# The opening of a float32 transformer block on one core: tokens also fetched as rows, four weight units in pieces, the strip product moved

## The chip, the cores and the metric

The kernel runs on one core of one Trainium2 chip. The metric is the device time of one execution in microseconds (us), the median of several runs.

## What is computed, cut to what matters

The input x has 512 tokens of 1024 channels, mem has 256 rows of 1024. The block is: a gated mixer with a short convolution, a long one and attention over mem; a convolutional feed-forward; an RMS norm; then a second layer of sliding-window attention with sinks and a bias per distance; a last RMS norm. The opening that the change touches computes this much of it:

```python
h    = rmsnorm(x, norm_mix_g)            # x * rsqrt(mean(x*x) + 1e-6) * g, over 1024 channels
memn = rmsnorm(mem, norm_mem_g)
k, v = split(memn @ w_kv)                # 256 x 2048
proj = h @ w_in                          # everything else of the mixer reads h
bias = t5_table[t5_bucket(distance)]     # second layer: one number per head and distance
```

## The kernel before, in words

**Units.** All weights stream from HBM in units of 128 x 1024 float32 (512 KB), four units a round, 54 rounds. Unit i uses slot i % 4 of three buffers: raw (w_raw), high (w_high) and low (w_low). Each float32 matmul is made of three with rounded operands: high x high, high x low of the activations, and low x high. ScalarE (ACT) makes the high part by a copy that rounds (round_high, L474; called by unit_high in the opening), VectorE (DVE) the low part by a subtraction (take_low, L1237; unit_low), TensorE (PE) multiplies. Channels lie on the partitions, tokens along the row, so x is eight tiles of 128 x 512 (x_in) and mem eight of 128 x 256.

**Who orders the work.** Every engine has a list written by hand and is in order; semaphores join them. SyncE (SP) issues the weights: in round m the load of slot s waits until the low part of the unit that had the slot is made (weight_low, L406). ACT's cast of unit i waits for its landing and until PE is done with unit i - 4 (unit_done). Nothing is reordered at run time: a step that waits holds up all that stands behind it on its engine.

**The opening.** Units 0 to 2 arrive in four pieces (CHUNKS) of 384 KB, each with two k tiles of all three units; mem arrives on ACT's queue in four pieces of 256 KB, with 4 KB of gains between, and 254 KB of other parameters behind. Unit 3 arrives whole. For each piece ACT rounds the three weight pieces (L519) and scales and rounds two tiles of mem (L525), DVE makes the low parts (L1326, L1332). PE runs four warm-up products of zeros (L964), then for each k tile nine matmuls of 256 columns (key_part, L927), and units 3 to 7 whole (key_unit, L939). Keys are divided by mem's norm later (take_k, L1350). The squares of mem are summed over tiles by ACT (L533) and DVE (L1343), and over channels by PE transposes (total, L909) and a DVE reduction. For x the same is done with eight squares on ACT (x_squares, L539), seven additions on DVE (add_x_squares, L1365) and four transposes on PE (L909, from part). spread (L917) turns the inverse roots back. Units 8 to 15 are the values (value_slab, L956). Meanwhile DVE scales the tiles of x (x_tiles: scale_tile L1274, low_tile L1279) and ACT rounds them (x_high, L505). The first round that reads h is two(R_LONG, 0, ...) (L872): it starts when units 16 and 17 are rounded and h's tiles arrive one by one. From there on PE has one long stream of products.

**The strip.** The distance bias of the second layer is a product of two small tables (L1089), made between the halves of the down projection, copied by DVE (L1675), stored by GpSimd (POOL), expanded in HBM, and read back.

Of the kernel before, what the change touches and what calls it, by code (L numbers as in the profile page):

```python
# [63 lines left out]
EARLY = 3  # L64
# [22 lines left out]
for _name, _n in (("g_mem", KT), ("g_mix", KT), ("long_w", KT * TAPS), ("long_b", KT), ("ln_g", KT), ("ln_b", KT),  # L87
                  ("gate_b", 3 * KT), ("short_w", 3 * KT), ("g_ffn", KT), ("ffn_w", 3 * 2 * F_TILES),
                  ("g_final", KT), ("g_second", KT), ("g_last", KT), ("sinks", HEADS_B)):
    PARAMS[_name] = _at  # L90
    _at += _n
# [6 lines left out]
def build(nc, weights, x, mem, params, consts, table, onehot, rows_g, out):  # L98
    with ExitStack() as ctx:
# [39 lines left out]
        mem_in = sb("mem_in", [P, KT, MEM], F32, 161)  # L139
        k_mem = sb("k_mem", [P, KT, MEM], F32, 161)  # L140
# [11 lines left out]
        x_sq = sb("x_sq", [P, KT, SEQ], F32, 64)  # L152
# [58 lines left out]
        strip = part[0:HEADS_B, 0, 0:2 * P]  # L211
        onehot_sb = convs[0:32, 0, 0:2 * P]
        table_sb = convs[0:32, 0, 2 * P:2 * P + HEADS_B]
        x_sum = part[:, 0, :]
# [17 lines left out]
        landed = [sem(f"weights_landed{s}") for s in range(SLOTS)]  # L232
        first_landed = [sem(f"first_landed{c}") for c in range(CHUNKS)]
        chunk_high = sem("chunk_high")
# [10 lines left out]
        x_squared = sem("x_squared")  # L245
        x_added = sem("x_added")
        gain_landed = sem("gain_landed")
# [114 lines left out]

        def stats(norm, n):


            return (slice(4, 4 + n), 2) if norm == N_MEM else (slice(0, n), 3)
# [29 lines left out]
        def _(sp):  # L396
            for c in range(CHUNKS):
# [4 lines left out]
            for s in range(EARLY, SLOTS):  # L402
                sp.dma_start(raw[s][:, :], weights[s]).then_inc(landed[s], 16)

            def load(m, s):
                sp.wait_ge(weight_low, 4 * m + (s - 3))  # L406
# [4 lines left out]

            load_x(0)
            load_x(1)
            load(1, 0)
            load(1, 1)
            load_x(2)
            load(1, 2)
            load_x(3)
            load(1, 3)
            with sp.Fori(2, ROUNDS) as m:  # L420
# [9 lines left out]
        def _(pool):  # L430
            pool.memset(conv_sum, 0.0).then_inc(zeros_set, 1)
            pool.dma_start(ones, consts[:, 0:P]).then_inc(consts_landed, 16)
# [3 lines left out]

            pool.wait_ge(ln_low, KT)
# [3 lines left out]
            pool.dma_start(table_sb, table).then_inc(tables_landed, 16)  # L441
            pool.dma_start(onehot_sb, onehot).then_inc(tables_landed, 16)
            pool.dma_start(own_keys[:, :], consts[:, 2 * P:3 * P]).then_inc(masks_landed, 16)
            pool.dma_start(older_keys[:, :], consts[:, 3 * P:4 * P]).then_inc(masks_landed, 16)
            pool.wait_ge(strip_ready, 1)
            pool.dma_start(strip_dram[:, :], strip).then_inc(strip_stored, 16)
            pool.wait_ge(strip_stored, 16)

# [16 lines left out]
        def _(act):  # L465
            def round_high(m, s):
# [3 lines left out]

                act.wait_ge(landed[s], 16 * m + (16 if s >= EARLY else 0))

                at_least(act, unit_done, 4 * m + (s - 3))
                act.activation(w_high[:, s, :], raw[s][:, :], ACT.Copy).then_inc(weight_high, 1)  # L474
# [32 lines left out]
            def load_memory(c):  # L507
                act.dma_start(mem_in[:, 2 * c:2 * c + 2, :], mem[:, 2 * c:2 * c + 2, :]).then_inc(mem_landed[c], 16)

            load_memory(0)  # L510
            act.dma_start(par[:, 0:KT], params[:, 0:KT]).then_inc(gain_landed, 16)
            for c in range(1, CHUNKS):
                load_memory(c)
            act.dma_start(par[:, KT:N_PARAMS], params[:, KT:N_PARAMS]).then_inc(par_landed, 16)
            for c in range(CHUNKS):
                act.wait_ge(first_landed[c], 16)
                for s in range(EARLY):
                    at = c * CHUNK
                    act.activation(w_high[:, s, at:at + CHUNK], raw[s][:, at:at + CHUNK], ACT.Copy)\  # L519
# [1419 lines left out]
```

## Time and profile before

| | us |
|---|---|
| three runs | 1213.33, 1213.44, 1213.69 |
| median | 1213.44 |
| profiled execution: its time | 1213.84 |
| profiled execution: its span | 1212.1 |
| PE busy | 1203.7 (99%) |
| DVE busy | 827.7 (68%) |
| ACT busy | 490.3 (40%) |

The span runs from the first to the last instruction of one profiled execution; its time has what lies around the span too. Busy time is summed per engine, and PE's matmuls overlap a little at their ends.

### The profile page before, as it was taken

How to read it: one execution, taken by the hardware profiler on the slowest of the kernel's cores; microseconds unless marked ns; L12 is line 12 of the kernel's file. 1: busy time of each engine (PE TensorE's matmuls, PEld its weight loads, DVE VectorE, ACT ScalarE, POOL GpSimd, SP SyncE). 2: the span in 40 equal slices, each digit the busy share in tenths (PEclk: the TensorE clock that was granted, in tenths of full speed). 3: DMA queues.
4: the chain of work that ended last, by engine and by line, in shares of the span. 5: the costliest groups of instructions: out<-in, count | busy, mean ns of one | idle time of the engine just before them, and what ended most of it. 6: DMA issues, size and time to landing. Idle time of an engine off the chain costs nothing.

```text
span 1212.1 us, 15930 instructions
## 1 busy us (share of the span) xinstructions
PE 1203.7 (99%) x5656; PEld 994.3 (82%) x5656; DVE 827.7 (68%) x1293; ACT 490.3 (40%) x785; POOL 7.5 (1%) x18
## 2 busy tenths in 40 slices
PE   9999999999999999999999999999999999999998
PEld 8888888888888888888887888888888888887786
DVE  6868897797889987553367866566654444578762
ACT  7544333232333323552244534334333333155643
POOL 0000000000000000000000000000000000000000
PEclk9999999999999999999999999999999999999999
DMA  8533222222222232243322222223233434221211
GB/s 321 179 104 104 87 104 83 74 87 87 70 87 90 100 105 87 87 174 104 104 87 87 90 104 92 96 104 104 87 110 104 174 104 139 87 71 53 74 66 70
DMA packets 35841, 125.51 MB, mean 104 GB/s; under 512 B 4080, under 2 KB 5760, under 8 KB 35536
## 3 DMA queue, kind: packets, MB, share of 16 engines
q1 hardware_dynamic: 33424, 116.41, 27.7%
q0 software_dynamic: 928, 6.08, 1.4%
q10 hardware_dynamic: 1440, 2.36, 0.5%
q8 instruction: 32, 0.52, 0.2%
q14 instruction: 17, 0.14, 0.0%
HBM read 122.72 MB, written 4.21 MB: 105 GB/s over the span
## 4 chain that ended last, share of the span: by engine, by line
PE 99%; DMA 0%; DVE 0%; ACT 0%; issue 0%; ACTq 0%; DVEq 0%
PE acc L855 80%; PE acc L872 3%; PE side L1203 2%; PE acc L1203 2%; PE acc L877 1%; PE acc L939 1%; PE side L1129 1%; PE acc L1167 1%; PE acc L892 1%; PE side L1005 1%; PE side L1025 1%; PE side L956 1%; PE acc L956 1%; PE acc L927 1%; PE acc L1139 1%; DMA par<-params 0%
## 5 line engine op out<-in xcount | busy, mean ns | idle before, releaser
L1237 DVE TENSOR_TENSOR w_low<-w_raw,w_high 128x1024 fp32r<-128x1024 f32 x213 | 257.6, 1221 | 42.1 <-ACT w_high L474 38.9
L474 ACT ACTIVATE w_high<-w_raw 128x1024 fp32r<-128x1024 f32 x213 | 221.0, 1051 | 103.2 <-PE acc L855 86.9
L855 PE MATMUL acc<-h_high,w_high 128*128 128x512 f32 x880 | 218.2, 390 | 0.0
L855 PE MATMUL acc<-h_low,w_high 128*128 128x512 f32 x880 | 217.4, 389 | 0.0
L855 PE MATMUL acc<-h_high,w_low 128*128 128x512 f32 x880 | 217.4, 390 | 0.0
L855 PEld LDWEIGHTS acc<-h_low,w_high 128*128 128x128 f32 x880 | 165.2, 188 | 34.3
L855 PEld LDWEIGHTS acc<-h_high,w_low 128*128 128x128 f32 x880 | 165.2, 188 | 34.2
L855 PEld LDWEIGHTS acc<-h_high,w_high 128*128 128x128 f32 x880 | 164.6, 188 | 33.8
L1312 DVE SCALAR_TENSOR_TENSOR convs<-long_u,par,convs 128x510 f32<-128x510 f32 (+28 forms) x232 | 170.4, 734 | 6.6
L1522 DVE TENSOR_TENSOR gate<-acc,gate 128x512 f32<-128x512 f32 x16 | 11.1, 692 | 53.7 <-PE acc L855 52.1
L855 PE MATMUL acc<-f_high,w_high 128*128 128x512 f32 x176 | 43.9, 390 | 0.0
L855 PE MATMUL acc<-f_low,w_high 128*128 128x512 f32 x176 | 43.8, 389 | 0.0
L855 PE MATMUL acc<-f_high,w_low 128*128 128x512 f32 x176 | 43.8, 389 | 0.0
L1654 DVE TENSOR_TENSOR x<-acc,x 128x512 f32<-128x512 f32 x8 | 5.5, 692 | 54.5 <-PE acc L855 54.5
L855 PEld LDWEIGHTS acc<-f_high,w_high 128*128 128x128 f32 x176 | 33.0, 188 | 7.2 <-issue 0.4
L855 PEld LDWEIGHTS acc<-f_high,w_low 128*128 128x128 f32 x176 | 33.0, 188 | 6.9
L855 PEld LDWEIGHTS acc<-f_low,w_high 128*128 128x128 f32 x176 | 33.0, 188 | 6.9
L635 ACT ACTIVATE ya_high<-part 128x512 fp32r<-128x512 f32 x8 | 5.1, 632 | 71.6 <-DVE part L1497 71.6
L738 ACT ACTIVATE square<-x 128x512 f32<-128x512 f32 x8 | 5.1, 632 | 70.8 <-DVE x L1654 70.8
L722 ACT ACTIVATE f_high<-part 128x512 f32 (+1 forms) x22 | 13.9, 632 | 48.3 <-DVE part L1636 48.3
L855 PE MATMUL acc<-xn_high,w_high 128*128 128x512 f32 x128 | 33.0, 400 | 0.0
L500 ACT ACTIVATE gate<-acc,par 128x512 f32<-128x512 f32 x24 | 16.5, 686 | 40.1 <-PE acc L855 40.0
(337 smaller groups left out, 1705.2 us busy)
## 6 DMA issues: line engine op xcount, KB each, us to landing
w_raw<-weights SPq DMA_DIRECT2D x213, 512.0 KB, 3.2
x_in<-x SPq DMA_DIRECT2D x4, 512.0 KB, 10.3
x<-x POOLq DMA_DIRECT2D x1, 2048.0 KB, 8.5
rows_dram<-strip_dram POOLq DMA_DIRECT2D x1, 2048.0 KB, 11.7
w_raw<-weights SPq DMA_DIRECT2D x4, 384.0 KB, 7.2
mem_in<-mem ACTq DMA_DIRECT2D x4, 256.0 KB, 7.3
bias<-rows_dram POOLq DMA_DIRECT2D x1, 1024.0 KB, 7.1
out<-result ACTq DMA_DIRECT2D x4, 256.0 KB, 2.6
```

What stands on the lines that cost most here:

```text
L474: act.activation(w_high[:, s, :], raw[s][:, :], ACT.Copy).then_inc(weight_high, 1)
L500: act.activation(gate[:, half, :], acc[:, 2 * half, :], ACT.Sigmoid, bias=0.0 if bias_col is None else bias_col).then_inc(taken[2 * half], 1)
L722: act.activation(f_high[:, j, :], part[:, half, :], ACT.Copy).then_inc(ffn_high, 1)
L855: mm = pe.matmul(acc[:, bank, 0:width], w[:, s, (skip + b) * P:(skip + b + 1) * P], moving[v][:, k, :], start=first and b == 0 and w is w_ ...
L872: pe.matmul(acc[:, s + i, 0:width], w_high[:, s + i, k * P:(k + 1) * P], moving[v][:, k, :], start=k == 0 and v == 0, stop=False)
L877: mm = pe.matmul(acc[:, s + i, 0:width], w_low[:, s + i, k * P:(k + 1) * P], moving[0][:, k, :], start=False, stop=k == KT - 1)
L892: mm = pe.matmul(acc[:, s + t // half, at:at + 2 * P], still[v][:, k, t * P:(t + 1) * P], w[:, s:s + 2, k * P:(k + 1) * P], start=k == 0 a ...
L927: mm = pe.matmul(acc[:, s, at:at + MEM], w[:, s, k * P:(k + 1) * P], memory[v][:, k, :], start=k == 0 and w is w_high and v == 0, stop=k = ...
L956: mm = pe.matmul(dst, o[:, k, t * P:(t + 1) * P], w[:, i, c * SEQ:(c + 1) * SEQ], start=k == 0 and o is mem_high and w is w_high, stop=k = ...
L1203: mm = pe.matmul(bank, o[:, k, t * P:(t + 1) * P], w[:, s, half * SEQ:(half + 1) * SEQ], start=False, stop=k == KT - 1 and o is o2_low)
L1237: dve.tensor_tensor(w_low[:, s, :], raw[s][:, :], w_high[:, s, :].bitcast(F32), ALU.subtract)\
L1312: dve.scalar_tensor_tensor(conv_acc[:, shift:SEQ], long_u[:, tile, 1:SEQ + 1 - shift], w, conv_acc[:, shift:SEQ], ALU.mult, ALU.add).then_ ...
```

## The change

In the opening all four units of the first round now arrive in pieces (EARLY is 4). Their first pieces of two k tiles are transfers of their own, 128 KB each, one per unit; the later three groups are 512 KB each. The very first weight piece is rounded by DVE instead of ACT. mem's gains are put in front of its first tile in one transfer (mem_first, 132 KB); the second tile and the next two come on ACT's queue, the other four on SP's between the weight groups; the 254 KB of parameters move to SP's queue, behind unit 9. PE's order within a group is unit by unit instead of tile by tile, and each pass waits for its own operands only. Units 4 and 5 get buffers of their own (w_spare), so that they are loaded without waiting for slots 0 and 1. Two of four warm-up products stay.

x is fetched a second time as rows, tokens on the partitions (x_rows, 2 MB, in SP's queue between units 8 and 9). ACT squares a row and sums along it in one instruction with accum_out (four of 128 x 1024). The eight squares, seven additions, PE's four transposes and DVE's reduction for x go.

The strip product runs on PE after the first group; its tables are POOL's first transfer, ACT copies the result and POOL stores it then. The order of the later steps of the opening on ACT, DVE and PE is rewritten.

The diff, cut to its core (from the third part on the added lines; unchanged and removed ones are left out):

```diff
 CHUNKS = 4
-EARLY = 3
+EARLY = SLOTS
+SPARE = 2
...
+        w_spare = sb("w_spare", [P, SPARE, UNIT], F32, 56)
+        x_rows = sb("x_rows", [P, SEQ // P, D], F32, 64)
...
+        def raw_of(m, s):
+            return w_spare[:, s, :] if isinstance(m, int) and m == 1 and s < SPARE else raw[s][:, :]
...
+        def mem_tile(k):
+            return mem_in[:, k, :] if k else mem_first[:, KT:KT + MEM]
...
+        def folds(norm):
...
+            return norm + (3 if norm == N_MEM else 2)
...
+            for s in range(EARLY):
+                sp.dma_start(w_raw[:, s, 0:CHUNK], weights[s, :, 0:CHUNK]).then_inc(alone_landed[s], 16)
+            for c in range(1, CHUNKS):
...
+                if c < CHUNKS - 1:
+                    tiles = slice(2 * c + 2, 2 * c + 4)
+                    sp.dma_start(mem_in[:, tiles, :],
+                                 mem[:, KT:KT + KT * MEM].rearrange("p (k n) -> p k n", k=KT)[:, tiles, :])\
+                      .then_inc(mem_landed[c + 1], 16)
+            for s in range(SPARE):
+                sp.dma_start(w_spare[:, s, :], weights[SLOTS + s]).then_inc(spare_landed[s], 16)
...
+            def load(m, s, units=None):
+                sp.wait_ge(weight_low, 4 * m + (s - 3) if units is None else units)
...
+            def load_rows(i):
+                sp.dma_start(x_rows[:, 2 * i:2 * i + 2, :],
+                             x_tokens.rearrange("(t p) d -> p t d", p=P)[:, 2 * i:2 * i + 2, :])\
+                  .then_inc(x_rows_landed[i], 16)
...
+            load(1, 2)
+            load(1, 3)
+            load(2, 0, 1)
+            load_rows(0)
+            load_rows(1)
+            load(2, 1, 2)
+            sp.dma_start(par[:, :], params).then_inc(par_landed, 16)
...
+            load(2, 2)
...
+            load(2, 3)
+            with sp.Fori(3, ROUNDS) as m:
...
+            pool.dma_start(tables_sb, tables).then_inc(tables_landed, 16)
...
+            act.dma_start(mem_first[:, :], mem[:, 0:KT + MEM]).then_inc(mem_first_landed, 16)
+            act.dma_start(mem_in[:, 1, :], mem[:, KT + MEM:KT + 2 * MEM]).then_inc(mem_landed[0], 16)
+            act.dma_start(mem_in[:, 2:4, :], mem[:, KT + 2 * MEM:KT + 4 * MEM].rearrange("p (k n) -> p k n", k=2))\
+               .then_inc(mem_landed[1], 16)
...
+                    if c or s:
+                        act.wait_ge(first_landed[c] if c else alone_landed[s], 16)
+                        act.activation(w_high[:, s, at:at + CHUNK], raw[s][:, at:at + CHUNK], ACT.Copy)\
+                           .then_inc(chunk_high if c < CHUNKS - 1 else weight_high, 1)
+                    if s == 0:
+                        for k in range(2 * c, 2 * c + 2):
+                            act.wait_ge(mem_landed[c] if k else mem_first_landed, 16)
+                            act.activation(mem_high[:, k, :], mem_tile(k), ACT.Copy, scale=mem_first[:, k:k + 1])\
+                               .then_inc(act_high, 1)
+            act.wait_ge(strip_done, 1)
+            act.activation(strip, side[0:HEADS_B, 2, 0:2 * P], ACT.Copy).then_inc(strip_ready, 1)
...
+            def x_squares(*tiles):
...
+                for t in tiles:
+                    act.wait_ge(x_rows_landed[t // 2], 16)
+                    act.activation(x_rows[:, t, :], x_rows[:, t, :], ACT.Square, accum_out=stat_col[:, t:t + 1])\
+                       .then_inc(x_summed, 1)
...
+            unit_high(4, 5, 6, 7, 8)
...
+            x_squares(0, 1)
+            unit_high(9)
+            x_squares(2, 3)
+            root(N_X)
...
+            unit_high(12)
+            x_high(2)
+            unit_high(13)
+            x_high(3)
+            unit_high(14)
+            x_high(4)
...
+            unit_high(15)
+            x_high(5)
+            unit_high(16)
+            x_high(6)
+            unit_high(17)
...
+            def key_part(c, i, by_tile):
...
+                passes = [(k, o) for k in range(2 * c, 2 * c + 2) for o in range(3)] if by_tile else \
+                    [(k, o) for o in range(3) for k in range(2 * c, 2 * c + 2)]
+                for k, o in passes:
+                    if o == 0:
+                        if c == 0 and i == 0:
+                            pe.wait_ge(first_high, 1)
+                        else:
+                            at_least(pe, *((chunk_high, EARLY * c + i) if c < CHUNKS - 1 else (weight_high, i + 1)))
+                        pe.wait_ge(act_high, k + 1)
+                    if o == 1:
+                        pe.wait_ge(act_low, k + 1)
+                    if o == 2:
+                        at_least(pe, *((chunk_low, EARLY * c + i + 1) if c < CHUNKS - 1 else (weight_low, i + 1)))
+                    w, v = ((w_high, 0), (w_high, 1), (w_low, 0))[o]
...
+                                   start=k == 0 and o == 0, stop=k == KT - 1 and o == 2)
+                if c == CHUNKS - 1:
...
+            for width in (SEQ, SEQ):
...
+            for c in range(CHUNKS):
...
+                    key_part(c, i, c == 0 and i == 0)
+                if c == 0:
+                    pe.wait_ge(tables_landed, 16)
+                    pe.matmul(side[0:HEADS_B, 2, 0:2 * P], tables_sb[:, 2 * P:2 * P + HEADS_B], tables_sb[:, 0:2 * P],
+                              start=True, stop=True).then_inc(strip_done, 1)
+            key_unit(4)
...
+            for i in range(5, KT):
+                key_unit(i)
...
+                if norm == N_X:
+                    dve.wait_ge(x_summed, n)
+                else:
+                    dve.wait_ge(stat_done, folds(norm))
+                    add_rows(cols, bank, n).then_inc(total_read, 1)
+                    dve.wait_ge(total_read, folds(norm))
...
+            dve.wait_ge(alone_landed[0], 16)
+            dve.tensor_copy(w_high[:, 0, 0:CHUNK], raw[0][:, 0:CHUNK]).then_inc(first_high, 1)
...
+                    if c == 0 and s == 0:
+                        dve.wait_ge(first_high, 1)
+                    elif c < CHUNKS - 1:
+                        dve.wait_ge(chunk_high, EARLY * c + s)
...
+                    for k in range(2 * c, 2 * c + 2) if s == 0 else ():
+                        dve.wait_ge(act_high, k + 1)
+                        dve.scalar_tensor_tensor(mem_low[:, k, :], mem_tile(k), mem_first[:, k:k + 1],
+                                                 mem_high[:, k, :].bitcast(F32), ALU.mult, ALU.subtract)\
+                           .then_inc(act_low, 1)
...
+            for c in range(1, CHUNKS):
+                add_mem_squares(c)
...
+            unit_low(4, 5, 6)
...
+            unit_low(7, 8, 9)
...
+            unit_low(10)
...
+            take_k(2, 6)
+            unit_low(11)
+            take_k(3, 7)
...
+            x_tiles(0, 1, 2)
+            unit_low(12)
+            x_tiles(3)
+            unit_low(13)
+            take_k(0, 4)
+            x_tiles(4)
+            unit_low(14)
+            x_tiles(5)
+            take_k(1, 5)
+            unit_low(15)
+            x_tiles(6, 7)
+            unit_low(16)
...
+            unit_low(17)
```

## Rows read from the trace of the kernel before

**Rows 1.** The page: chain that ended last, and the DMA issues of weight units.
```profile
PE 99%; DMA 0%; DVE 0%; ACT 0%; issue 0%; ACTq 0%; DVEq 0%
...
w_raw<-weights SPq DMA_DIRECT2D x213, 512.0 KB, 3.2
```

**Rows 2.** Timeline of PE and its weight loads (PEld): start, duration, count.
```profile
1.32 5.88 PE L964 MATMUL side<-convs 128*128 128x512 f32 x8 [1.32 <-POOL convs L431]
...
4.05 0.34 PEld L964 LDWEIGHTS side<-convs 128*128 128x128 f32 x1 [0.52 <-issue]
...
6.60 0.19 PEld L964 LDWEIGHTS side<-convs 128*128 128x128 f32 x1 [0.51 <-issue]
...
8.23 0.36 PE L927 MATMUL acc<-mem_high,w_high 128*128 128x256 f32 x1 [1.03 <-DVE mem_low L1332]
...
19.81 1.12 PE L939 MATMUL acc<-mem_high,w_high 128*128 128x256 f32 x8
...
31.54 0.60 PE L909 MATMUL side<-ident_sb,part 128*128 128x128 f32 x4
31.98 0.38 PE L917 MATMUL side<-ident_sb,root_col 128*128 128x128 f32 x2
...
54.81 0.47 PE L872 MATMUL acc<-h_high,w_high 128*128 128x512 f32 x1 [0.18 <-ACT w_high L474]
```

**Rows 3.** Timeline of PE around the strip product.
```profile
950.28 0.60 PE L1089 MATMUL side<-convs 32*16 32x256 f32 x2
950.81 2.11 PE L855 MATMUL acc<-f_high,w_high 128*128 128x512 f32 x8
```

**Rows 4.** Windows: stretch, length, busy us by engine, PE clock, DMA share, GB/s.
```profile
5.00:10.00 5.00, 3.96 (x20) 2.56 (x19) 3.49 (x10) 4.07 (x11) 0.00 (x0) 1.00 1.04 360
10.00:15.00 5.00, 5.00 (x44) 5.00 (x43) 4.25 (x11) 4.28 (x11) 0.00 (x0) 1.00 1.05 400
15.00:20.00 5.00, 5.00 (x44) 5.00 (x43) 3.78 (x5) 4.76 (x9) 0.00 (x0) 1.00 0.97 351
20.00:25.00 5.00, 5.00 (x44) 5.00 (x44) 4.31 (x6) 3.72 (x6) 0.00 (x0) 1.00 1.02 414
...
35.00:40.00 5.00, 5.00 (x26) 4.20 (x25) 4.96 (x8) 1.11 (x2) 0.00 (x0) 1.00 0.63 214
40.00:45.00 5.00, 5.00 (x24) 4.14 (x23) 5.00 (x10) 2.68 (x4) 0.00 (x0) 1.00 0.34 97
```

**Rows 5.** DMA issues at 0.75, 0.76, 1.24, 2.84 and 16.61: KB, us to landing.
```profile
w_raw<-weights SPq DMA_DIRECT2D x1, 384.0 KB, 4.9
mem_in<-mem ACTq DMA_DIRECT2D x1, 256.0 KB, 4.4
...
par<-params ACTq DMA_DIRECT2D x1, 4.0 KB, 5.7
...
w_raw<-weights SPq DMA_DIRECT2D x1, 512.0 KB, 11.0
...
w_raw<-weights SPq DMA_DIRECT2D x1, 512.0 KB, 8.9
```

**Rows 6.** Timeline of ACT and its queue (ACTq).
```profile
1.79 1.62 ACTq L508 DMA_DIRECT2D mem_in<-mem  x3
...
5.68 1.03 ACT L519 ACTIVATE w_high<-w_raw 128x256 fp32r<-128x256 f32 x3 [0.38 <-DMA w_raw<-weights]
6.98 0.91 ACT L525 ACTIVATE mem_high<-mem_in,par 128x256 fp32r<-128x256 f32 x2 [0.27 <-DMA par<-params]
...
15.24 2.18 ACT L533 ACTIVATE mem_sq<-mem_in 128x512 f32<-128x512 f32 x4
...
52.61 1.99 ACT L474 ACTIVATE w_high<-w_raw 128x1024 fp32r<-128x1024 f32 x2
```

**Rows 7.** Timeline of DVE: units 10 and 11, and the scaling of tile 6.
```profile
35.82 2.35 DVE L1237 TENSOR_TENSOR w_low<-w_raw,w_high 128x1024 fp32r<-128x1024 f32 x2
...
51.30 0.74 DVE L1274 SCALAR_TENSOR_TENSOR part<-x_in,par,side 128x512 f32<-128x512 f32 x1
```

More of the change, by code:

```diff
@@ L95, with build @@
 N_MEM, N_X, N_LN, N_FFN, N_FINAL, N_LAST = range(-2, 4)
-def build(nc, weights, x, mem, params, consts, table, onehot, rows_g, out):
+def build(nc, weights, x, x_tokens, mem, params, consts, tables, rows_g, out):
     with ExitStack() as ctx:
@@ L210, in build @@
         ffn_y = [gate[:, 0, :], gate[:, 1, :], conv_acc, conv_sum]
[L211 to L214, printed above, removed]
+        strip = probs[0:HEADS_B, 0, :]
+        tables_sb = convs[0:32, 0, 0:2 * P + HEADS_B]
         rstd_mem = gate[:, 0, 0:MEM]
@@ L232, in build @@
         landed = [sem(f"weights_landed{s}") for s in range(SLOTS)]
+        alone_landed = [sem(f"alone_landed{s}") for s in range(EARLY)]
         first_landed = [sem(f"first_landed{c}") for c in range(CHUNKS)]
+        spare_landed = [sem(f"spare_landed{s}") for s in range(SPARE)]
+        first_high = sem("first_high")
+        mem_first_landed = sem("mem_first_landed")
+        x_rows_landed = [sem(f"x_rows_landed{i}") for i in range(2)]
+        x_summed = sem("x_summed")
         chunk_high = sem("chunk_high")
@@ L469, in round_high @@
                     return
-                act.wait_ge(landed[s], 16 * m + (16 if s >= EARLY else 0))
+                if isinstance(m, int) and m == 1 and s < SPARE:
+                    act.wait_ge(spare_landed[s], 16)
+                else:
+                    act.wait_ge(landed[s], 16 * m - (16 if s < SPARE else 0))
                 at_least(act, unit_done, 4 * m + (s - 3))
-                act.activation(w_high[:, s, :], raw[s][:, :], ACT.Copy).then_inc(weight_high, 1)
+                act.activation(w_high[:, s, :], raw_of(m, s), ACT.Copy).then_inc(weight_high, 1)
             def ahead(m, s):
@@ L1086, in _ @@
             down_body(0)
-            pe.wait_ge(tables_landed, 32)
-            pe.matmul(side[0:HEADS_B, 2, 0:2 * P], table_sb, onehot_sb, start=True, stop=True)\
-              .then_inc(strip_done, 1)
             down_body(1)
@@ L1673, in _ @@
             down_body(0)
-            dve.wait_ge(strip_done, 1)
-            dve.tensor_copy(strip, side[0:HEADS_B, 2, 0:2 * P]).then_inc(strip_ready, 1)
             down_body(1)
```

148 lines of the change are left out of this document (21 added, 127 removed).

## The prediction

> **What bounds the kernel now.** I read four views, in this order. The page's chain that ended last is 99% TensorE (PE) [rows 1]. So a change of the opening pays only through PE: a later or earlier first useful matmul, PE work removed, PE waits removed or added. PE's order of time shows where its stream begins: warm-up matmuls from 1.32 to 7.20 us, the first useful matmul at 8.23, then no gap until 54.81, where the first round that reads h (L872) waits 0.18 us for ScalarE's (ACT's) cast of a weight unit [rows 2]. Third, the other engines beside it: VectorE (DVE) is busy 4.96 and 5.00 us of the two 5 us stretches from 35 to 45 us [rows 4]; it is nearly the bound there, and the 0.18 us wait is its shadow, since ACT's cast of units 16 and 17 stands behind a tile of h that DVE has to scale. Fourth, the DMA view: the core's queues are full, 400 and 414 GB/s, in the stretches from 10 and from 20 us [rows 4].
>
> This makes three clocks: PE's, the DVE/ACT chain's, and that of the loads. The kernel before is paced by the first, with the second 0.2 us behind. The profiled execution took 1213.84 us around its span of 1212.1; the median of the three runs is 1213.44. Sums are made against the profiled one, then 0.40 is taken off.
>
> **PE's own gains.** (a) The transposes of the sum of x squares go: from 31.54 to the next group at 31.98, 0.44 us [rows 2]. (b) The strip product leaves the down projection: its two instructions stand between 950.28 and 950.81, 0.53 us [rows 3]. It is added after the first pieces in the opening. There PE will wait anyway (below), so I cost it at nothing there; without that cover it costs the same 0.53 back, and (b) is zero. (c) The number of key and value matmuls is the same, 192 and 96 groups' worth, only in another order.
>
> **PE's start.** Now the first matmul waits for the whole first piece of three units and for the 4 KB of gains, which landed 5.7 us after their issue at 1.24, hence 6.95; then come two ACT steps (the first from 6.98) and two of DVE [rows 5, 6]. After the change the first transfers are 128 and 132 KB instead of 384 and 256 KB; these landed 4.9 and 4.4 us after issue [rows 5], at 5.65 and 5.16. With a third of the bytes ahead I take 4.1 us for both. Bounds: an uncontended 512 KB unit lands 3.2 us after issue [rows 1], of which 1.27 are its bytes at 414 GB/s; a quarter of the bytes would land at 0.75 + 1.9 + 0.3 = 3.0; no gain gives 5.2. ACT's table load is out of the way by then, because ACT issues three transfers ahead of it instead of six, at 0.54 us each [rows 6]. One DVE copy of 0.4 and one ACT piece of 0.5 follow, and the two warm-up matmuls (four instructions of 0.85 us, from 1.32 [rows 2]) end at 4.75. First matmul: 4.85 us, 3.4 earlier.
>
> **What of this lasts.** PE then needs the pieces in time. Before the second group of pieces is complete, 1024 KB on SP's queue, 516 on ACT's and 163 on POOL's must land, 1703 KB. Before the fourth group it is 3239 KB (2560 on SP's). Before the change unit 3 landed at 2.84 + 11.0 = 13.84 [rows 5] behind 3458 KB (2048, 1282, 128). The 219 KB less are 0.55 us at 400 GB/s: fourth group at 13.3. The second stands 1536 KB (1.57 MB) ahead of it; at 360 to 400 GB/s [rows 4] that is 4.1 us: 9.2, and adding up the rate rows forwards gives 8.5; I take 9.0. Group 1 keeps PE busy until about 8.6, and then it waits, with the strip product inside the wait. ACT needs for a group four weight pieces at 0.34 and two of mem at 0.46 [rows 6], 2.2 us, so ACT ends groups 2 to 4 at 11.2, 13.4 and 15.6. PE needs 24 matmuls at 0.12 (96 took from 8.23 to 19.81 [rows 2]) = 2.88 us a group. Its first unit of group 2 is done at about 11.2, a step behind ACT's and DVE's pieces of mem; the other three units end at 13.4, group 3 at 16.3, group 4 at 19.2. Unit 4 is the next wait. Its cast now stands behind the strip copy (0.4) and all squares of mem (2.4, four took 2.18 [rows 6]): 15.6 + 2.8 + 1.05 = 19.5. Before, unit 4 began at 19.81 [rows 2]. So of 3.4 us only 0.3 are left here. With (a), PE would be ready for the h round at 54.63 - 0.3 - 0.44 = 53.9.
>
> **What the loads allow.** The change adds 2 MB (x again, as rows), in SP's queue ahead of units 9, 10 and 11, and moves the 254 KB of parameters there. Unit 6 is loaded when three units' low parts are done: ACT's third piece of group 4 plus DVE's 0.42, about 15.7 us; POOL's queue is not in the way, as it only issues its 163 KB first and then waits for the strip. An uncontended unit lands 3.2 us after issue [rows 1]: 18.9. From there to the landing of unit 11 are 13.5 pieces of 512 KB (units 7 to 11: 5, rows 4, x 4, parameters 0.5). Two prices for one: at 414 GB/s, the rate from 20 to 25 us [rows 4], 1.27 us; from landing to landing, 13.84 to 16.61 + 8.9 = 25.51 for eight pieces [rows 5], 1.46, which has a dip of the rate in the 5 us from 15 in it (351 GB/s [rows 4]). I take 1.31, the 400 GB/s row, because it is the nearest stretch with one queue full and no dip; 17.7 us, so unit 11 lands at 36.6 (36.0 to 38.6).
>
> The Trainium skill, page "DMA: Bandwidth & Descriptors", section "Anatomy of one DMA — SWDGE (gpsimd) path", gives 436 GB/s for the part that grows with size. By it a piece is 1.20 us, unit 11 lands at 35.1 and the sum below would end PE-bound. The trace's best 5 us show 414.
>
> **What DVE then needs.** DVE takes unit 11's low part ahead of every tile of h, in an in-order queue. Before, from the start of unit 10's low part (35.82) to the scaling of tile 6 (51.30) it ran 15.48 us without a gap: six low parts, six scalings, five h lows, four K tiles [rows 7]. After, from unit 11's: one low part less (1.14), two K tiles more (0.67): 15.0. From that scaling the way to PE was ACT's h tile, two casts, and PE at 54.81 [rows 2, 6]; with the new interleave it is one cast: 52.61 + 1.05 + 0.21 - 51.30 = 2.6. With the cast of unit 11 ahead (1.1) the h round starts 18.7 us after unit 11 has landed: 36.6 + 18.7 = 55.3. That DVE no longer adds x squares (seven of them) doesn't help: this work lay before the landing, and the time becomes idling for weights. ACT's squares of rows (four of twice the length, for eight at 0.54) lie there too.
>
> **Sum.** The h round starts at 55.3 instead of 54.81: +0.5. Afterwards PE's stream is as before, its loads are far ahead, and the strip is out: -0.53. Together 0.0. The other moves cost nothing: the strip's store and POOL's early wait lie 140 us ahead of the first reader (attend), which has one more satisfied wait; mem's gains travel with mem. 1213.84 + 0.0 - 0.40 = 1213.4; with the landing at 36.0, which the 1.27 price gives, it is 1212.8, and I take 1213.3.
>
> **Rivals.**
> 1. PE stays the pace: the loads keep up (unit 11 by 35.2 or earlier) and the whole gain of the opening stays. Then the h round starts when PE is ready, 53.9: -0.91 - 0.53 = -1.4, so 1212.0; if the second group lands at 8.0 instead of 9.0 and ACT follows, one more us, 1211.0. For it: 414 GB/s over five us, and a DVE with spare time before 33 us. Against: 2 MB ahead of weights in one queue, and a gap of about 1 us in the queue before unit 6. Chance 0.28; a third of it is beyond 2.4 us.
> 2. The other side: the loads fall behind. At 1.46 us a piece unit 11 lands at 38.6, the h round starts at 57.3: +2.5 - 0.53 = +2.0, so 1215.4; it decides once a piece takes over 1.31. Past 1.49 it is slower by over 0.2%. For it: the measured eight landings. Chance 0.14, half of it past the bound.
> 3. The clock. The first warm-up instructions (512 columns) start 0.85 us apart (three between 4.05 and 6.60) and their weight loads take 0.34 us; the one at 6.60 takes 0.19 [rows 2], as do all later ones. That is the step from 1.2 to 2.4 GHz, although the granted-clock column shows 1.00 throughout [rows 4]; PE had been busy for about 5 us. The change halves this warm-up and follows it with matmuls that wait. At 1.2 GHz a 256-column matmul takes 0.21 instead of 0.12. Group 1 slow costs 24 x 0.09 = 2.2 us, of which a third is covered by the wait for group 2, and what is left by the 1.4 us that PE waits at the h round; only when group 2 is slow too is PE late, by 2 us: 1215.3. The Trainium skill, page "TensorE: Matmul & The Clock Gate", Part 1, says that the low level is the default and activity lifts it, which speaks against cutting the warm-up; by that rule, the trace agrees that it began low. Chance 0.08, a third of it past the bound.
> 4. The strip product isn't covered, or the squares of rows are late for the spread at about 33.5 us: some tenths, inside the range.
>
> **How the numbers follow.** The forecast case (loads gate the h round, 1212.4 to 1214.2) has 0.50, rivals 1, 2, 3 have 0.28, 0.14, 0.08. A measurement of this kernel can tell about 0.2%, 2.4 us, from no change. Faster by more: a third of rival 1 and a bit, 0.10. Slower by more: half of rival 2 and a third of 3, 0.10. Within: 0.80. The range reaches from rival 1's far end, 1211.2, to rival 2's 1215.3.
>
> **What would show it.** First matmul near 4.9 us; a PE wait of 0.5 to 1 us before its second group; unit 4 at about 19.5; no L909 from part; DVE idle 5 us or more between 24 and 37 us behind casts that wait for DMA; unit 11's landing at 36 to 37; a wait of over 1 us at the h round for ACT's cast, at about 55.3; no strip instruction near 950. Wrong if PE's wait at the h round is absent (rival 1), if the landing is past 38 (rival 2), or if weight loads of 0.34 us are still seen after 9 us (rival 3).

## The result, and the profile after

| | before | after |
|---|---|---|
| median of 15 runs each, us | 1213.47 (1213.33 to 1214.14) | 1215.58 (1215.03 to 1216.68) |
| ratio, 95% interval | | 1.0019 (1.0012 to 1.0025) |
| profiled execution: time, span, us | 1213.84, 1212.1 | 1215.88, 1214.1 |
| first useful matmul, us | 8.23 | 4.70 |
| unit 4 on PE, us | 19.81 | 19.15 |
| first round that reads h, us | 54.81 | 57.66 |

The kernel became 2.1 us slower. That is a little less than the 2.4 us (0.2%) which the prediction took as the least that one measurement can tell, but it is outside the predicted range (1211.2 to 1215.3) by 0.3 us. The interval of the ratio lies above 1, so the loss is real.

The page's chain of the kernel after, which answers to [rows 1], and then PE's waits (engine, line, releaser: us in all, times, longest):

```profile
PE 95%; DMA 2%; DVE 2%; ACT 1%; issue 0%; SPq 0%; DVEq 0%; ACTq 0%
```

```profile
PE acc L1007 <- ACT w_high L509: 1.8, 1, 1.8
...
PE acc L912 <- ACT w_high L509: 1.2, 1, 1.2
...
PE side L1007 <- ACT w_high L509: 0.3, 1, 0.3
```

Before, 99% of the chain was PE. Now 5% lie elsewhere, 2% of the span with the loads of weights: DMA, ACT's cast and DVE's low part have become links of the chain. All three waits are for a cast of a weight unit. The timeline of PE says when; it answers to [rows 2] and [rows 3]:

```profile
1.32 3.78 PE L1015 MATMUL side<-convs 128*128 128x512 f32 x4 [1.32 <-POOL convs L464]
4.70 0.61 PE L978 MATMUL acc<-mem_high,w_high 128*128 128x256 f32 x1
...
9.21 0.60 PE L1021 MATMUL side<-convs 32*16 32x256 f32 x2
9.96 0.76 PE L978 MATMUL acc<-mem_high,w_high 128*128 128x256 f32 x2
...
19.15 1.12 PE L990 MATMUL acc<-mem_high,w_high 128*128 128x256 f32 x8
...
40.23 1.19 PE L1007 MATMUL side<-w_high,mem_high 128*128 128x512 f32 x4 [0.30 <-ACT w_high L509]
...
45.08 1.20 PE L1007 MATMUL acc<-w_high,mem_high 128*128 128x512 f32 x4 [1.83 <-ACT w_high L509]
...
57.66 0.47 PE L912 MATMUL acc<-h_high,w_high 128*128 128x512 f32 x1 [1.23 <-ACT w_high L509]
```

The front of the opening is what was forecast: the useful work starts 3.5 us earlier, and of that 0.66 us are left at unit 4. Everything is lost between 40 and 58 us, in three waits of 3.4 us together: 0.30 at unit 11, 1.83 at unit 12 and 1.23 at the h round (the first round that reads h). The ledger against the kernel before has three entries. The h round starts 57.66 - 54.81 = 2.85 us later. By 949 us 0.09 of that has worn off: the product at 951.36 is the one that stood at 948.60 before. Then the strip's two instructions are missing. Before the change, first, and after it, these are the products around the place (those at 950.28 and 950.81 are in [rows 3]):

```profile
948.60 1.75 PE L855 MATMUL acc<-f_high,w_low 128*128 128x512 f32 x7
...
952.76 1.98 PE L855 MATMUL acc<-f_low,w_high 128*128 128x512 f32 x8
```

```profile
951.36 1.75 PE L895 MATMUL acc<-f_high,w_low 128*128 128x512 f32 x7
952.95 1.98 PE L895 MATMUL acc<-f_high,w_high 128*128 128x512 f32 x8
954.76 1.98 PE L895 MATMUL acc<-f_low,w_high 128*128 128x512 f32 x8
```

The same products take 3.40 us now and took 4.16, so the strip was worth 0.76 us there, not only the 0.53 between its own start and the next product's. The sum is 2.85 - 0.09 - 0.76 = +2.0, by which the spans differ.

Why the casts are late shows on ACT and DVE, after (start, duration; the bracket is the idle time before and what ended it). The three casts are those of units 9, 10 and 11, the low part is unit 11's:

```profile
29.50 1.06 ACT L509 ACTIVATE w_high<-w_raw 128x1024 fp32r<-128x1024 f32 x1 [1.63 <-DMA w_raw<-weights]
...
35.28 1.06 ACT L509 ACTIVATE w_high<-w_raw 128x1024 fp32r<-128x1024 f32 x1 [1.99 <-DMA w_raw<-weights]
39.12 1.06 ACT L509 ACTIVATE w_high<-w_raw 128x1024 fp32r<-128x1024 f32 x1 [2.78 <-DMA w_raw<-weights]
```

```profile
40.21 1.22 DVE L1280 TENSOR_TENSOR w_low<-w_raw,w_high 128x1024 fp32r<-128x1024 f32 x1 [1.49 <-ACT w_high L509]
...
42.02 1.40 DVE L1320 SCALAR_TENSOR_TENSOR part<-x_in,par,side 128x512 f32<-128x512 f32 x2
```

Each cast starts within 0.1 us of its unit's landing. DVE stands behind unit 11 too: only after its low part does it scale the first tile of h, at 42.02. Before the change unit 11's low part was done at 38.2, since it is the second of the two that start at 35.82 [rows 7]. SP's queue and the issue of unit 11 (KB, us to landing) close the chain backwards:

```profile
15.87 2.35 SPq L430 DMA_DIRECT2D w_raw<-weights  x3
18.26 0.94 SPq L436 DMA_DIRECT2D x_rows<-x_tokens  x2
```

```profile
w_raw<-weights SPq DMA_DIRECT2D x1, 512.0 KB, 14.0
```

Unit 11 is issued at 25.05 and lands at 39.05. Before the change a unit in the full queue took 8.9 and 11.0 us [rows 5]. The windows of 2 us around SP's issue show one more thing; the columns are those of [rows 4]:

```profile
12.00:14.00 2.00, 2.00 (x19) 2.00 (x19) 2.00 (x7) 1.96 (x7) 0.00 (x0) 1.00 1.06 394
14.00:16.00 2.00, 2.00 (x19) 2.00 (x18) 2.00 (x7) 2.00 (x7) 0.00 (x0) 1.00 0.50 199
16.00:18.00 2.00, 2.00 (x19) 2.00 (x18) 1.06 (x3) 2.00 (x6) 0.51 (x1) 1.00 0.58 152
18.00:20.00 2.00, 2.00 (x19) 2.00 (x19) 1.86 (x4) 2.00 (x4) 0.00 (x0) 1.00 0.87 258
```

From 14 to 20 us only 199, 152 and 258 GB/s move, where the stretches around show 394 and 398. The queue has run dry: a shorter window shows that nothing moves from 15.5 to 16.0, and it fills again only slowly.

```profile
15.50:16.00 0.50, 0.50 (x6) 0.50 (x6) 0.50 (x3) 0.50 (x3) 0.00 (x0) 1.00 0.00 0
```

SP stands at the load of unit 6, which waits for the low parts of three units (weight_low) until 15.87. Behind it in SP's list are the 2 MB of rows, which wait for nothing.

### The profile page after: what moved, and what is told of

It reads as the page before. It is cut to its first block, busy times and chain, and to the rows that moved or that the text cites. A ratio compares the mean times of both kernels' runs of the same rounds, so it can differ in the third digit from the quotient of the medians.

```text
span 1214.1 us, 15903 instructions
## 1 busy us (share of the span) xinstructions
PE 1203.3 (99%) x5648; PEld 993.5 (82%) x5648; DVE 823.1 (68%) x1288; ACT 491.2 (40%) x789; POOL 7.0 (1%) x17
## 4 chain that ended last, share of the span: by engine, by line
PE 95%; DMA 2%; DVE 2%; ACT 1%; issue 0%; SPq 0%; DVEq 0%; ACTq 0%
PE acc L895 80%; PE acc L912 3%; DMA w_raw<-weights 2%; PE side L1246 2%; PE acc L1246 2%; PE acc L917 1%; PE side L1172 1%; PE acc L1210 1%; PE acc L932 1%; PE side L1052 1%; PE side L1072 1%; DVE w_low L1280 1%; PE acc L1182 1%; PE side L1062 0%; DVE part L1320 0%
## 5 line engine op out<-in xcount | busy, mean ns | idle before, releaser
L1280 DVE TENSOR_TENSOR w_low<-w_raw,w_high 128x1024 fp32r<-128x1024 f32 x210 | 254.3, 1221 | 45.9 <-ACT w_high L509 42.6
L509 ACT ACTIVATE w_high<-w_raw 128x1024 fp32r<-128x1024 f32 x210 | 218.4, 1051 | 107.9 <-PE acc L895 86.2
L1563 DVE TENSOR_TENSOR gate<-acc,gate 128x512 f32<-128x512 f32 x16 | 11.1, 692 | 53.7 <-PE acc L895 52.2
```

The source lines that it names most:

```text
L509: act.activation(w_high[:, s, :], raw_of(m, s), ACT.Copy).then_inc(weight_high, 1)
L1280: dve.tensor_tensor(w_low[:, s, :], raw_of(m, s), w_high[:, s, :].bitcast(F32), ALU.subtract)\
```

## Experiments, first set: what sets the h round

The theory after the result was that the h round is unit 11's landing plus a fixed chain, and that the landing is late by 2 MB in a queue that had been empty for some microseconds. The rivals were a slow clock after the halved warm-up, and ACT's list (the squares of the rows stand ahead of the casts).

**rows_first** issues the rows ahead of the waiting load.

```diff
+            load_rows(0)
+            load_rows(1)
             load(1, 2)
             load(1, 3)
             load(2, 0, 1)
-            load_rows(0)
-            load_rows(1)
```

> Both transfers of x as rows (2 MB) are issued before the load of unit 6, which waits for weight_low 3; nothing else changes. Load theory (the queue runs empty from about 15.3 to 18 us while SP stands at that wait, and the landing of unit 11 sets the h round 18.6 us later): the queue stays full, unit 11 lands about 2.3 us earlier, at 36.8 instead of 39.1, PE's waits before units 10 and 12 go, the h round starts at 55.4 instead of 57.66, the time falls by 2.2 us to 1213.4; unit 6 lands near 22 instead of 19.8, which PE doesn't need before 24.9. Clock theory (the loss is matmuls at 1.2 GHz at the start): no change, 1215.6.

Measured: 1213.31 us (1213.03 to 1213.75, 11 runs), ratio 0.9999 (0.9990 to 1.0008). The move of two lines gives back the whole loss. First the same windows of 2 us, then from the timeline ACT's cast of unit 11, DVE's low part of it, and PE's h round:

```profile
14.00:16.00 2.00, 2.00 (x19) 2.00 (x18) 2.00 (x6) 2.00 (x7) 0.00 (x0) 1.00 1.03 412
16.00:18.00 2.00, 2.00 (x19) 2.00 (x18) 1.06 (x3) 2.00 (x6) 0.51 (x1) 1.00 1.03 410
18.00:20.00 2.00, 2.00 (x19) 2.00 (x19) 1.86 (x4) 1.91 (x3) 0.00 (x0) 1.00 1.02 403
```

```profile
35.69 1.06 ACT L509 ACTIVATE w_high<-w_raw 128x1024 fp32r<-128x1024 f32 x1 [0.31 <-DMA w_raw<-weights]
...
37.68 1.22 DVE L1280 TENSOR_TENSOR w_low<-w_raw,w_high 128x1024 fp32r<-128x1024 f32 x1
...
55.12 0.47 PE L912 MATMUL acc<-h_high,w_high 128*128 128x512 f32 x1 [0.92 <-ACT w_high L509]
```

The dip is gone, and unit 11 is cast 3.4 us earlier. The h round gains only 2.5 us: now 2.0 us pass between that cast and DVE's low part, without a wait of DVE, where in the kernel after it was 1.1. So another gate has come up close behind the landing. Unit 6 lands later (cast at 23.53, after 3.62 us of waiting), and PE doesn't notice. So units 6 to 8 need not go ahead of the rows.

**half_rows** takes 1 MB of rows, two pieces of 512 KB, out of the queue. ACT squares the rows of the first half a second time in place of those of the second (into a buffer rows_out, which is new), so its work is the same and the statistics of the second half of the tokens are left out. **extra_load** puts 512 KB more in, behind the rows, into a buffer that no product reads (ACT waits for it behind the values, long after it has landed).

```diff
-            load_rows(1)
...
-                    act.wait_ge(x_rows_landed[t // 2], 16)
-                    act.activation(x_rows[:, t, :], x_rows[:, t, :], ACT.Square, accum_out=stat_col[:, t:t + 1])\
+                    act.wait_ge(x_rows_landed[0], 16)
+                    act.activation(x_rows[:, t, :] if t > 1 else rows_out[:, t, :], x_rows[:, t % 2, :], ACT.Square, accum_out=stat_col[:, t:t + 1])\
```

> Only the first half of x as rows is fetched (1 MB less ahead of units 9 to 11); the squares of token tiles 2 and 3 are taken from tiles 0 and 1 again, so the statistics of the second half of the tokens are left out. Work on every engine is the same. Load theory: unit 11 lands 2.6 us earlier, at 36.5, the h round starts at about 55.1, time 1213.1. Clock theory: no change, 1215.6. If the cost were ACT's squares of rows and not the bytes: no change either.

```diff
             load_rows(1)
+            sp.dma_start(extra[:, :], weights[8]).then_inc(extra_landed, 16)
             load(2, 1, 2)
```

> One more 512 KB transfer (a copy of unit 8 into an unused buffer) behind the rows in SP's queue. Load theory: each later landing moves by 1.3 to 1.4 us and passes to the end one to one: 1216.9. Theory that PE or DVE work bounds the opening: no change, 1215.6.

Measured, both 0.5 us above what was expected: half_rows 1213.61 us (1212.55 to 1214.15), ratio 1.0001 (0.9992 to 1.0010); extra_load 1217.36 (1216.67 to 1217.91, 6 runs), ratio 1.0032 (1.0020 to 1.0045). Their casts of unit 11 and h rounds, first half_rows and then extra_load:

```profile
37.12 1.06 ACT L509 ACTIVATE w_high<-w_raw 128x1024 fp32r<-128x1024 f32 x1 [4.31 <-DMA w_raw<-weights]
...
55.70 0.47 PE L912 MATMUL acc<-h_high,w_high 128*128 128x512 f32 x1 [1.26 <-ACT w_high L509]
```

```profile
41.19 1.06 ACT L512 ACTIVATE w_high<-w_raw 128x1024 fp32r<-128x1024 f32 x1 [2.77 <-DMA w_raw<-weights]
...
59.73 0.47 PE L916 MATMUL acc<-h_high,w_high 128*128 128x512 f32 x1 [1.22 <-ACT w_high L512]
```

ACT's work is the same in half_rows and the loss is gone all the same, so the squares of the rows aren't the cause; the bytes are.

**warm4** has the four warm-up products of the kernel before.

```diff
-            for width in (SEQ, SEQ):
+            for width in (SEQ, SEQ, SEQ, MEM):
```

> All four warm-up products again, so PE is busy with them until about 7.2 us and starts the first group 2.4 us later, at 2.4 GHz. Load theory: PE starts late but the h round still waits for unit 11, 57.7: time within 0.3 us of 1215.6, PE's waits before units 10, 12 and the h round shorter by what it starts later. Clock theory: the slow matmuls go, faster by 1 us or more, 1214.6 or less.

Measured: 1215.70 us (1214.83 to 1216.81), ratio 1.0020 (1.0011 to 1.0029); unit 4 at 19.26. It is as slow as the kernel after, so the clock of the first microseconds isn't the cause. PE's first useful matmul comes at 6.26, not 2.4 us later than in the kernel after but 1.6, and the strip, right behind group 1, at 9.40 instead of 9.21: what PE loses by the later start, it gets back by the faster products.

The four kernels in one table (us; the last column is the h round less the start of DVE's low part of unit 11):

| | cast of unit 11 | h round | difference | from DVE's low part |
|---|---|---|---|---|
| half_rows | 37.12 | 55.70 | 18.58 | 17.48 |
| after | 39.12 | 57.66 | 18.54 | 17.45 |
| extra_load | 41.19 | 59.73 | 18.54 | 17.45 |
| rows_first | 35.69 | 55.12 | 19.43 | 17.44 |

The landing moves over 4 us and the h round follows it one for one. In warm4 (and in strip_twice, below) SP's list is that of the kernel after, and yet unit 11 is cast at 38.77 and 38.54; the h rounds, at 57.31 and 57.09, are again 18.54 and 18.55 us behind. So the landing itself differs by 0.6 us between executions of one list, and differences of that size between these kernels say nothing of their edits. In rows_first the cast no longer decides, but DVE's low part still does, to 0.04 us. The chain from there on is DVE's own work, as [rows 7] said.

## Experiments, second set: the next gate, and a better version

In rows_first the landing of unit 11 cost only 0.31 us. The theory was now that the lists of ACT, DVE and PE hold the casts of units 10 and 11 back. In the kernel after, the casts wait for PE to be done with unit i - 4, ACT has the last two squares and the root of x between the casts of units 9 and 10, and DVE takes x's mean between the low parts of 9 and 10.

**loads_only** improves only SP's list further (x after units 10 and 11 where it can), with the other lists as they are.

```diff
+            load_rows(0)
+            load_rows(1)
             load(1, 2)
             load(1, 3)
             load(2, 0, 1)
-            load_rows(0)
-            load_rows(1)
             load(2, 1, 2)
...
+            load(2, 2)
             load_x(0)
+            load(2, 3)
             load_x(1)
-            load(2, 2)
             load_x(2)
             load_x(3)
-            load(2, 3)
```

> On top of rows_first the loads of units 10 and 11 also move ahead of most of x in SP's queue; ACT, DVE and PE keep the order of the changed kernel. Load theory taken alone (unit 11's landing sets the h round): unit 11 lands about 3.5 us earlier than in rows_first, near 32, so the h round would start when PE is ready, 54.2, and the time would be 1212.4. List theory (once the queue is full, ACT's list is next: unit 10 is cast only after four squares and the root, so DVE starts its low part at 35.4 as in rows_first): the h round stays at about 55.1, time 1213.3.

Measured: 1213.24 us (1213.17 to 1213.79), ratio 1.0000 (0.9991 to 1.0009). ACT, DVE and PE of this kernel:

```profile
34.19 1.99 ACT L509 ACTIVATE w_high<-w_raw 128x1024 fp32r<-128x1024 f32 x2
...
37.53 1.22 DVE L1280 TENSOR_TENSOR w_low<-w_raw,w_high 128x1024 fp32r<-128x1024 f32 x1
...
54.97 0.47 PE L912 MATMUL acc<-h_high,w_high 128*128 128x512 f32 x1 [0.91 <-ACT w_high L509]
```

ACT now casts 10 and 11 back to back and waits for no transfer, and yet they begin at 34.19: both units lie ready. The h round is 17.44 us after DVE's low part once more. Earlier landings alone gain nothing more that can be measured; the lists hold.

**reordered** adds to loads_only what the lists need: all four squares of rows right after unit 5, both roots after unit 8, both means together on DVE, and PE's spread of x's root ahead of the first value slab.

```diff
-            unit_high(4, 5, 6, 7, 8)
-            root(N_MEM, MEM // P)
-            x_squares(0, 1)
-            unit_high(9)
-            x_squares(2, 3)
-            root(N_X)
-            unit_high(10, 11)
+            unit_high(4, 5)
+            x_squares(0, 1, 2, 3)
+            unit_high(6, 7, 8)
+            root(N_MEM, MEM // P)
+            root(N_X)
+            unit_high(9, 10, 11)
...
-            value_slab(0, 0)
             spread(N_X, SEQ)
+            value_slab(0, 0)
...
             mean_square(N_MEM, MEM)
-            unit_low(7, 8, 9)
             mean_square(N_X, SEQ)
+            unit_low(7, 8, 9)
             unit_low(10)
```

> As loads_only, and ACT squares all four row tiles right after unit 5, takes both roots after unit 8, DVE makes both mean squares together, PE spreads x's roots ahead of unit 8's product. The work is the same. List theory: DVE reaches the tiles of h some 3 us earlier, PE is the pace with no wait at the h round, which starts at about 53.7: -1.1 against before there and -0.53 for the strip: 1211.8. If some other bound lies behind (PE's own start, DVE's sum of work), the h round stays near 55 and the time above 1213.

Measured: 1211.89 us (1211.49 to 1213.13), ratio to the kernel before 0.9988 (0.9979 to 0.9997). It is faster than both kernels: 3.7 us less than after, 1.5 less than before. The cast of unit 11, and PE at the h round:

```profile
33.62 1.06 ACT L509 ACTIVATE w_high<-w_raw 128x1024 fp32r<-128x1024 f32 x1 [2.37 <-DMA w_raw<-weights]
...
52.72 1.07 PE L1006 MATMUL acc<-w_low,mem_high 128*128 128x512 f32 x4
53.62 0.39 PE L911 MATMUL acc<-h_high,w_high 128*128 128x512 f32 x1
```

There is no bracket at 53.62: PE goes from the last product of the values straight into the h round, and PE is the bound again. What PE still waits for behind its first product is 0.25 us at group 2 and 0.24 us at unit 6. The cast of unit 11 waits for its landing again, but 33.62 + 18.54 is 52.2, and PE isn't ready before 53.62. The four moves came together; no run shows which of them could be left out.

**reordered_warm4** is that kernel with four warm-up products, since the clock might have been covered by the waits until now.

> As reordered, with four warm-up products instead of two. Here PE should be the pace, so that a PE start that is later, but at 2.4 GHz, can show. Clock theory: faster than reordered by 0.3 us or more. Theory that the wait for the second group of pieces absorbs either: equal within 0.2 us.

Measured: 1211.82 us (1211.47 to 1212.23), ratio 0.9987 (0.9978 to 0.9996): no different from reordered. PE starts group 1 at 5.89 instead of 4.63, the strip at 9.04 instead of 8.91, and reaches unit 4 at 19.02 instead of 18.97. The halved warm-up costs nothing that can be measured.

**strip_twice** makes the strip product twice in the opening of the kernel after.

```diff
+                    pe.matmul(side[0:HEADS_B, 2, 0:2 * P], tables_sb[:, 2 * P:2 * P + HEADS_B], tables_sb[:, 0:2 * P],
+                              start=True, stop=True)
                     pe.matmul(side[0:HEADS_B, 2, 0:2 * P], tables_sb[:, 2 * P:2 * P + HEADS_B], tables_sb[:, 0:2 * P],
                               start=True, stop=True).then_inc(strip_done, 1)
```

> The changed kernel with the strip product issued twice in the opening, same operands and target. If PE's wait for the second group of pieces (and the later waits for units 10 to 17) cover it: 1215.6, no change. If the strip product lies on the path there: plus 0.45 us, 1216.0.

Measured: 1215.62 us (1215.27 to 1217.0), ratio 1.0021 (1.0012 to 1.0030), against 1.0019 for the kernel after. A second product costs nothing either: the place is covered in that kernel, by the waits behind it. In reordered, where PE waits less, it wasn't tried; its trace shows PE idle for 0.25 us between the strip at 8.91 and group 2 at 9.76, for ACT's cast of a tile of mem, so one strip product is covered there too.

## Why the prediction failed, step by step

The forecast case was that the loads gate the h round. They do, and the price of the chain behind the landing was right. What failed is the term for the landing itself, which was mis-sized by 2.45 us, and with it the choice between the forecast case and rival 2.

- **PE's own gains.** Right in kind: the transposes from part are gone, and so is the strip at 950. The strip's gain was 0.76 and not 0.53, since its two neighbours got shorter as well. Rival 4 fell: a second strip product cost nothing in strip_twice, and PE doesn't wait for the roots at 33.9 in the kernel after.
- **PE's start.** Forecast 4.85, measured 4.70; unit 4 forecast 19.5, measured 19.15. The wait ahead of group 2 was to be 0.5 to 1 us; from the strip at 9.21 to group 2 at 9.96 it is 0.75 us with the strip inside. Groups 2 to 4 end at 13.39, 16.27 and 19.15, forecast 13.4, 16.3 and 19.2. Group 1 took 4.5 us instead of 2.9, but the sum had put a wait behind it that covered this. Only the cast of unit 4, at 17.92, came earlier than the sum had it, and PE didn't wait for it.
- **PE ready for the h round at 53.9.** Reordered shows it without a wait ahead: 53.62.
- **What DVE then needs, 18.7 us from the landing.** Right: 57.66 - 39.05 = 18.6, and the table above holds it over 4 us of landing.
- **What the loads allow: the step that failed.** Unit 11 was to land at 36.6 and landed at 39.05, outside its bounds of 36.0 to 38.6. The 2.45 us come from four places. Unit 6 was issued at 15.87 instead of 15.7 (+0.17). It took 3.7 us instead of the 3.2 of an uncontended unit (+0.5). Units 7 and 8 landed at 21.4 and 22.95, 3.4 us for two pieces instead of 2.6 (+0.8), while SP was still issuing them, unit 8 only at about 17.8. And the 11.5 pieces from unit 8 to unit 11 took 16.1 us, 1.40 each on average instead of 1.31 (+1.0); the table below shows that this is one late landing and not a slower queue. The text had the average of the kernel before, 1.46, as a bound, and took the rate of a window [rows 4] instead, on the ground that the stretch of the average had a dip in it. Per piece from unit 6 on it became 19.5 / 13.5 = 1.44: the new kernel had slow stretches too, and its sum had no term for them.
- **Sum.** With 39.05 the prediction's own sum gives 39.05 + 18.7 - 54.81 - 0.53 = +2.4; measured +2.1, and the strip's 0.76 is most of the difference. That is rival 2, which was priced at 1215.4 with a chance of 0.14; the median is 1215.58. Its mechanism, that the loads fall behind, is right. Its price of 1.46 us for every piece is right only on average, and that two kernels with different losses have nearly the same average is luck.
- **Rival 1** (PE stays the pace, 1212.0) is wrong for this kernel and right for reordered, 1211.89: the change holds that gain, if the lists let it.
- **Rival 3** (the clock) fell twice, with warm4 and reordered_warm4. Its mechanism is there, see the last section, but group 1 took 1.6 us more and not 2.2, and group 2 was fast.
- **Not seen ahead.** PE waits not once but three times: ahead of the h round 0.30 at unit 11, and 1.83 at unit 12, whose cast stands in ACT's list behind the first tiles of h. They cost nothing of their own: without them PE would have waited that much longer at the h round, which DVE's chain sets.

Rival 1 named a gap of about 1 us in the queue ahead of unit 6; that the queue would run dry for longer, and fill slowly, wasn't forecast. The text put the rows into SP's list behind the waiting load, as the change does, and counted their bytes from unit 6's landing; it didn't ask what else the queue could carry while SP waits. rows_first shows that this is where the whole loss can be had back.

When each transfer landed tells more than the averages (us; each is the issue plus the time to landing):

| | after | rows_first |
|---|---|---|
| unit 6 | 19.6 | 23.5 |
| unit 7 | 21.4 | 24.8 |
| unit 8 | 23.0 | 26.1 |
| rows, first and second half | 25.6, 28.2 | 18.5, 22.2 |
| unit 9 | 29.5 | 27.3 |
| parameters | 30.1 | 28.0 |
| x, first and second quarter | 31.4, 32.7 | 29.3, 30.6 |
| unit 10 | 35.3 | 31.9 |
| x, third and fourth quarter | 36.5, 37.8 | 33.1, 34.4 |
| unit 11 | 39.1 | 35.7 |

In rows_first the 9.5 pieces from unit 6 to unit 11 land in 12.2 us, 1.28 each, which is what the windows' 404 to 411 GB/s give. In the kernel after nearly all steps in the full queue are 1.28 too. Two things are lost on top. Unit 5 lands at 15.9 and unit 8 at 23.0: three units take 7.0 us where 1.28 each would make 3.8. That is the dry queue, and it is worth 3.2 us. And from the second quarter of x to unit 10 it is 2.6 us for one piece, although the queue is busy. The two issues, at 20.92 and 23.19, and what moved from 32.7 to 35.26:

```profile
x_in<-x SPq DMA_DIRECT2D x1, 512.0 KB, 11.8
...
w_raw<-weights SPq DMA_DIRECT2D x1, 512.0 KB, 12.1
```

```profile
DMA packets 284, 1.04 MB, mean 405 GB/s; under 512 B 31, under 2 KB 31, under 8 KB 284
```

Two pieces' worth of bytes moved while one piece landed. rows_first has such a late landing as well, between its two halves of rows (3.7 us for two pieces), and the kernel before has two, of 1.8 and 2.3 us, among the eight that made its 1.46; their other six steps are 1.25 to 1.28. Nor was the queue of the kernel before ever dry there: in the lowest half microsecond from 14 to 21, that from 18.5, it still moved 197 GB/s.

This also explains why 512 KB more cost 2.1 us in extra_load and 1 MB less saved only 2.0 in half_rows. In extra_load unit 8, ahead of the extra transfer, already landed 0.9 us late, at 23.9, and the piece added 1.3. In half_rows two pieces saved 2.6, and two slower steps took back 0.5.

Left open is what makes a landing late. By 39.05 the core had moved 8.5 MB since 15.87 (the windows' rates times their lengths), while the pieces up to unit 11 are 14.5, or 7.6 MB. The difference, 0.9 MB, fits units 12 to 14, issued at 26.3, 32.0 and 37.8. So it looks as if bytes of later transfers went ahead of the last ones of unit 11, but no run shows the order within the 16 engines.

## What to carry to other kernels

In the list of an engine that issues transfers in order, put those that wait for nothing ahead of one that waits; here two moved lines were worth 2.3 us. Read a full queue landing by landing, and not by one average. Here the usual step was 1.28 us per 512 KB, as the windows' rate says; what broke the forecast stood beside it, 3.2 us for a queue that ran dry and 1.3 for one late landing. A sum needs a term of its own for each, or the average of the old kernel as its bad case. When a gate is moved and the time gains less than the gate did, look for the next one in the lists: here loads alone reached 1213.2, loads and lists together 1211.9.

## What the runs showed of the hardware

The granted clock of the profile is 1.00 in every window shown, yet PE begins at half rate. Weight loads of the kernel after, then matmuls in pairs:

```profile
3.19 0.34 PEld L1015 LDWEIGHTS side<-convs 128*128 128x128 f32 x1 [0.52 <-issue]
...
6.16 0.34 PEld L978 LDWEIGHTS acc<-mem_high,w_low 128*128 128x128 f32 x1
```

```profile
7.01 0.60 PE L978 MATMUL acc<-mem_low,w_high 128*128 128x256 f32 x2
7.44 0.41 PE L978 MATMUL acc<-mem_high,w_low 128*128 128x256 f32 x2
7.69 0.40 PE L978 MATMUL acc<-mem_high,w_high 128*128 128x256 f32 x2
```

From 7.01 to the next pair it is 0.43 us, from 7.44 on 0.24 to 0.25: the step from 1.2 to 2.4 GHz, 0.21 and 0.12 us for a matmul of 256 columns. The first group of 24 matmuls takes 4.5 us, from 4.70 to 9.21, instead of 2.9. The step doesn't come at one time. In the kernel before, the load at 5.75 is the last slow one and that at 6.60 the first fast one [rows 2]; in reordered_warm4, where PE is busy from 1.32 on with the same four products, the first fast one is at 4.79. First the kernel before, then reordered_warm4:

```profile
5.75 0.34 PEld L964 LDWEIGHTS side<-convs 128*128 128x128 f32 x1 [0.52 <-issue]
```

```profile
4.79 0.19 PEld L1014 LDWEIGHTS side<-convs 128*128 128x128 f32 x1 [0.41 <-issue]
```

The slow products cost nothing in the end: part of the loss went into the wait for group 2, and four warm-up products don't make reordered faster.

The second thing is the gap between moved and landed. Windows of the kernel after, columns as in [rows 4]:

```profile
25.00:30.00 5.00, 5.00 (x44) 5.00 (x43) 1.16 (x2) 3.25 (x7) 0.00 (x0) 1.00 1.03 415
30.00:35.00 5.00, 5.00 (x31) 4.30 (x29) 1.57 (x3) 2.84 (x6) 0.00 (x0) 1.00 1.02 406
35.00:40.00 5.00, 4.93 (x22) 3.76 (x20) 2.31 (x4) 1.94 (x2) 0.00 (x0) 1.00 1.01 390
```

They move 390 to 415 GB/s, while, with the one late landing among them, the 11.5 pieces from unit 8 to unit 11, 6.03 MB, landed in 16.1 us, which is 374 GB/s. The Trainium skill, page "DMA: Bandwidth & Descriptors", section "Why a DMA increments its semaphore by 16 and not by 1", says that a transfer runs on up to 16 engines that finish independently and has landed only when each has reported. By that a landing is the slowest engine's, and the others can be in the next transfers by then; the numbers here agree with it, and no run shows the engines one by one.

The same page, section "Where 436 GB/s comes from", also says that loads from HBM are bound at about 358 GB/s per core. The windows here show up to 415 GB/s from HBM to the core's memory over 5 us, so that bound doesn't hold in this trace. As a price of landings it would give an estimate of 1.46 us a piece. The usual step was 1.28, which is 410 GB/s; the average of 1.44 comes near the estimate only because it holds the slow refill and the late landing. The 1.20 us of the figure that the prediction weighed is a little under every step that the table shows in full queue.
